# Two halved norms: GpSimd makes one half of slot 1's weight remainder, the vector engine the other, and slot 1's matmuls follow all of slot 0's

## The reference, cut to what matters

```
x  = x  + 0.5 * gate * swiglu(modulate(rms_norm(x,  g), shift, scale), w_in, w_out)   # latent tokens
xc = xc + 0.5 * gate * swiglu(modulate(rms_norm(xc, g), shift, scale), w_in, w_out)   # context tokens
hx = modulate(rms_norm(x, g1), ...);  hc = modulate(rms_norm(xc, g1), ...)
q, k, v = split(h @ w_qkv)      # differential attention: q of the latents, k and v of both
```

## Time and profile before

| | before |
|---|---|
| median of 3 runs | 2273.41 us (2270.28 to 2276.93) |
| the profiled execution | 2277.63 us, span 2274.6 us |
| TensorE busy | 2234.0 us (98%) |
| vector engine busy | 1460.7 us (64%) |
| ScalarE busy | 847.1 us (37%) |
| GpSimd busy | 161.4 us (7%) |
| granted TensorE clock | 0.993 of full speed |

### The profile page before, as it was taken

One profiled execution on the slowest core, in us unless ns is written; L12 is line 12 of the kernel. 1 busy time (PEld: TensorE's weight loads), 2 busy tenths in 40 slices (PEclk: granted clock), 3 DMA queues, 4 the chain that ended last, 5 costly groups with the idle time before them and its releaser, 6 DMA issues.

```text
span 2274.6 us, 37311 instructions
## 1 busy us (share of the span) xinstructions
PE 2234.0 (98%) x14124; PEld 2009.0 (88%) x14124; DVE 1460.7 (64%) x2305; ACT 847.1 (37%) x1133; POOL 161.4 (7%) x235
## 2 busy tenths in 40 slices
PE   8999999999999999999999999999999999999998
PEld 8999999999999988888988888898888888788998
DVE  4657886555788777678777767873333346556555
ACT  4445344444635432122432212232212234445443
POOL 0100000130000100010001001100000001000000
PEclk9999999998999999999999999999999999999999
DMA  6325664323665555455245555533232223113453
GB/s 229 113 80 207 207 229 155 135 78 120 211 239 185 194 194 179 175 191 178 91 149 201 171 177 193 175 116 111 79 106 102 81 95 130 56 57 131 179 201 136
DMA packets 65482, 343.19 MB, mean 151 GB/s; under 512 B 7152, under 2 KB 10480, under 8 KB 42608
## 3 DMA queue, kind: packets, MB, share of 16 engines
q1 hardware_dynamic: 44656, 266.47, 33.4%
q0 software_dynamic: 20736, 75.51, 9.9%
HBM read 340.90 MB, written 1.05 MB: 150 GB/s over the span
## 4 chain that ended last, share of the span: by engine, by line
PE 81%; issue 11%; DVE 4%; ACT 3%; DMA 1%; POOL 0%; DVEq 0%; SPq 0%; ACTq 0%; POOLq 0%
PE gpt L868 20%; PE gpt L869 20%; PE gpt L870 20%; ACT w_hi L1492 2%; DVE w_lo L1999 1%; PE gpt L967 1%; PE mbt L1150 1%; PE gpt L789 1%; PE gpt L790 1%; PE gpt L791 1%; PE gpt L968 1%; PE gpt L969 1%; PE mbt L1409 1%; PE gpt L1367 1%; PE gpt L1368 1%
## 5 line engine op out<-in xcount | busy, mean ns | idle before, releaser
L868 PE MATMUL gpt<-xn_hi,w_hi 128*128 128x512 f32 (+2 forms) x2256 | 745.3, 330 | 6.4 <-DVE midf L2210 3.6
L870 PE MATMUL gpt<-xn_hi,w_lo 128*128 128x512 f32 (+2 forms) x2256 | 740.8, 328 | 0.0
L869 PE MATMUL gpt<-xn_lo,w_hi 128*128 128x512 f32 (+2 forms) x2256 | 740.8, 328 | 0.0
L1999 DVE TENSOR_TENSOR w_lo<-raw,w_hi 128x2048 fp32r<-128x2048 f32 (+2 forms) x277 | 560.8, 2025 | 238.7 <-ACT w_hi L1492 238.7
L1492 ACT ACTIVATE w_hi<-raw 128x2048 fp32r<-128x2048 f32 (+2 forms) x277 | 471.2, 1701 | 368.5 <-PE gpt L870 324.7
L868 PEld LDWEIGHTS gpt<-xn_hi,w_hi 128*128 128x128 f32 x2256 | 426.1, 189 | 47.4 <-DVE midf L2210 6.0
L870 PEld LDWEIGHTS gpt<-xn_hi,w_lo 128*128 128x128 f32 x2256 | 426.2, 189 | 37.2
L869 PEld LDWEIGHTS gpt<-xn_lo,w_hi 128*128 128x128 f32 x2256 | 425.4, 189 | 37.6
L868 PE MATMUL gpt<-mid_hi,w_hi 128*128 128x512 f32 (+2 forms) x996 | 331.3, 333 | 5.2 <-DVE mid_lo L2215 4.0
L869 PE MATMUL gpt<-mid_lo,w_hi 128*128 128x512 f32 (+2 forms) x996 | 330.0, 331 | 0.0
L870 PE MATMUL gpt<-mid_hi,w_lo 128*128 128x512 f32 (+2 forms) x996 | 330.0, 331 | 0.0
(11 more groups left out here) (345 smaller groups left out, 2706.8 us busy)
## 6 DMA issues: line engine op xcount, KB each, us to landing
raw<-in_up_a SPq DMA_DIRECT2D x72, 1024.0 KB, 4.8
ada_w<-in_ada POOLq DMA_DIRECT2D x144, 512.0 KB, 3.5
raw<-in_up_b SPq DMA_DIRECT2D x60, 1024.0 KB, 4.7
raw<-in_down_a SPq DMA_DIRECT2D x48, 768.0 KB, 4.3
raw<-in_down_b SPq DMA_DIRECT2D x48, 640.0 KB, 3.9
raw<-in_win SPq DMA_DIRECT2D x16, 1024.0 KB, 4.9
raw<-in_qkv SPq DMA_DIRECT2D x12, 1024.0 KB, 4.8
raw<-in_wout SPq DMA_DIRECT2D x8, 1024.0 KB, 4.8
```

Of the source, the lines that this page charges most:

```text
L868: mm(o, wh[b][:, j, :], hi(k), start=(k == 0), stop=False)
L869: mm(o, wh[b][:, j, :], lo(k), start=False, stop=False)
L870: last = mm(o, wl[b][:, j, :], hi(k), start=False, stop=(k == kt - 1))
L1999: V.tensor_tensor(wl[b][:, 0:tiles, :], raw[b][:, 0:tiles, :], wh[b][:, 0:tiles, :].bitcast(F32), ALU.subtract).then_inc(lo_ready, 1)
```

## The change: what it does

GpSimd gets a new step, `second_low`, between its two powers at norms 7 and 8: when ScalarE has rounded slot 1, it subtracts the half of the remainder with k below 4 (128x1024). The vector engine's whole remainder of slot 1 goes; instead it makes the other half, `second_split`, behind latent tile 7, after a wait for GpSimd's half. Its order becomes: remainders of tiles 2 and 3 with tiles 4 and 5, the context half's means, tiles 6 and 7, its half of the remainder, the context tiles. TensorE does all of slot 0 first, with the context half's columns in its middle, then slot 1 with tiles 0 to 3 after a wait for GpSimd's half, the context half's rows, and slot 1 with tiles 4 to 7 after a wait for the vector engine's half. Norm 6 keeps the old order.

```
             def half_powers(ni, low=None):
                 for c in range(2):
+                    if c == 1 and low is not None:
+                        second_low(low)
...
+            def second_low(s):
+                pool.wait_ge(hi_ready, s + 1)
+                nc.gpsimd.tensor_tensor(by_k(w_lo[1], 0), by_k(raw[1], 0), by_k(w_hi[1], 0).bitcast(F32), ALU.subtract)\
+                    .then_inc(second_lo, 1)
...
-            half_powers(7)
-            half_powers(8)
+            half_powers(7, S_F4 + 1)
+            half_powers(8, S_QKV + 1)
...
                 if after != POOL_NORM:
                     half_columns(after, 1)
-                else:
-                    pool_sums(1, range(6, KT))
+                    gemm_part(0, hi, lo, 0, range(4, KT), xn_ready, r0, done)
+                    pe.wait_ge(second_lo, after - 6)
+                    pe.wait_ge(evac_done, free_at(2 * p + 1))
+                    gemm_part(1, hi, lo, 0, range(0, 4), xn_ready, r0)
+                    half_rows(after, 1)
+                    pe.wait_ge(lo_ready, done_at(2 * p + 1))
+                    gemm_part(1, hi, lo, 0, range(4, KT), xn_ready, r0, done)
+                    return
+                pool_sums(1, range(6, KT))
...
+            def second_split(p, n):
+                dve.wait_ge(second_lo, n)
+                V.tensor_tensor(by_k(w_lo[1], 1), by_k(raw[1], 1), by_k(w_hi[1], 1).bitcast(F32), ALU.subtract).then_inc(lo_ready, 1)
...
-            norm2_half(7, 0, range(2, KT // 2), 4)
-            split(S_F4 // 2, 1, SIDE_T)
+            norm2_half(7, 0, range(2, KT - 2), 4)
             half_columns(7, 1)
-            norm2_half(7, 0, range(KT // 2, KT))
+            norm2_half(7, 0, range(KT - 2, KT))
+            second_split(S_F4 // 2, 1)
             norm2_half(7, 1, range(KT))
```

More of the change, by code:

```diff
@@ L264, in build @@
         first_hi, first_lo = sem("first_hi"), sem("first_lo")
-        k_hi, k_lo = sem("k_hi"), sem("k_lo")
+        k_hi, k_lo, second_lo = sem("k_hi"), sem("k_lo"), sem("second_lo")
         half_done, res_x, xq_ready, xs_used = sem("half_done"), sem("res_x"), sem("xq_ready"), sem("xs_used")
@@ L653, in _, with half_powers @@
             load_ada(2)
-            def half_powers(ni):
+            def second_low(s):
+                pool.wait_ge(hi_ready, s + 1)
+                nc.gpsimd.tensor_tensor(by_k(w_lo[1], 0), by_k(raw[1], 0), by_k(w_hi[1], 0).bitcast(F32), ALU.subtract)\
+                    .then_inc(second_lo, 1)
+            def half_powers(ni, low=None):
                 for c in range(2):
+                    if c == 1 and low is not None:
+                        second_low(low)
                     pool.wait_ge(hpart_ready, half_chain(ni, c) + 1)
@@ L2721, in _ @@
                 late=[lambda w=w: derive(1, w) for w in range(3)])
-            norm2_half(7, 0, range(2, KT // 2), 4)
-            split(S_F4 // 2, 1, SIDE_T)
+            norm2_half(7, 0, range(2, KT - 2), 4)
             half_columns(7, 1)
-            norm2_half(7, 0, range(KT // 2, KT))
+            norm2_half(7, 0, range(KT - 2, KT))
+            second_split(S_F4 // 2, 1)
             norm2_half(7, 1, range(KT))
             ffn(S_F4 // 2, 4, T2, gated_residual(1, 0, T2), [SIDE_T, SIDE_T], 8, 3)
-            norm2_half(8, 0, range(2, KT // 2), 4)
-            split(S_QKV // 2, 1, SIDE_T)
+            norm2_half(8, 0, range(2, KT - 2), 4)
             half_columns(8, 1)
-            norm2_half(8, 0, range(KT // 2, KT))
+            norm2_half(8, 0, range(KT - 2, KT))
+            second_split(S_QKV // 2, 2)
             norm2_half(8, 1, range(1))
```

## The result

The changed kernel took 2287.4 us in the median of 9 runs (2282.07 to 2292.78), the kernel before, on the same chip, 2275.55 (2270.28 to 2280.65). The ratio is 1.0049, with a 95% interval of 1.0034 to 1.0064: 11.2 us slower, 7.7 to 14.6.

A forecast was written before the change was run, and what follows sets the result against it. TensorE, busy 98%, bounds the kernel, so only its pauses count. 2.8 us without a collision plus 2 x 1.9 of hold make 6.6 us slower: 2280.0 on the runs' median, own range 2277 to 2284, outer range 2274.0 to 2287.0.

The forecast's parts named there:

- The hold: Norms 7 and 8: GpSimd's half holds the vector engine's tile 2 remainder, 1.9 us each; whole hold 0.70.
- my four multiplies: Length of GpSimd's 128x1024 half, taken as four 128x256 multiplies: 2.5 us.
- Norm 8's restart: Second query slot: TensorE goes on 6.39 us after the context half's rows, 2.5 us later than before.
- the late rows: Norm 8: second half's rows, moved behind 24 more matmuls, set the chain to the query slot; 2.5 us.
- Norm 7 without the collision: Ahead of the fourth feed-forward: the new order gives nothing back, costing 0.2 us plus 0.1 at the context tiles.
- the collision: Norms 7 and 8: GpSimd's half and tile 2's remainder contend, lengthening TensorE's pause; 2 x 1.9 us.
- A partial hold: Rival: the vector engine slips in between GpSimd's pieces; half the hold, 4.7 us slower; chance 0.15 with no hold.
- no hold: Rival: GpSimd's half doesn't hold tile 2's remainder; 2.8 us slower, 2276.2; chance 0.15 with a partial hold.
- A far slower GpSimd: Rival: rounded output doubles GpSimd's half to 5 us, holding 4.4 at each norm; 11.7 us slower; chance 0.10.
- The faster one: Rival: with w_lo off the vector engine, 2.21 us go at both norms; 4.4 us less, 2269.0; chance 0.05.
- That the change doesn't act: Rival: late ScalarE rounding moves the hold to tile 3 at about the same price; counted in the first case.
- the bound between them: About 0.3% (6.8 us), what a measurement can tell from no change; the forecast lay just inside.

The follow-up runs named there:

- experiment 1: The changed kernel with GpSimd's half given back to the vector engine, TensorE's new order kept; ratio 1.0025 to the kernel before.
- experiment 3: The changed kernel with nine unused keep_clock calls filling TensorE's pause between tiles 1 and 2; ratio 1.0023 to the kernel before.
- experiment 2: The kernel before, old order, with slot 1's remainder cut in two and the first half on GpSimd; ratio 1.0040 to the kernel before.
- experiment 5: experiment 1 with the second half's rows made right behind slot 0's last tile; ratio 0.9998 to the kernel before.
- experiment 6: The kernel before with two unused vector-engine subtractions ahead of tile 2's remainder, no GpSimd half; ratio 1.0034, 7.7 us slower.

## Why the prediction was right and wrong

**The hold: right, sizes a little high.** GpSimd's half took 2.34 (I took 2.5). It held tile 2's remainder for 1.72 (I had 1.9) and lengthened the pause by as much. The Trainium skill (SBUF — State Buffer, "Who interferes with whom") says that the first to issue keeps the shared ports for the whole instruction; the trace agrees, as the remainder lost 1.72 of the 1.92 us that it stood beside one GpSimd instruction of 2.34. The estimate of 2.25, half of what the Trainium skill (GPSIMD Engine Reference, "Elementwise — side-by-side cycle accounting") has for 2048 elements, was nearer than my four multiplies.

**Norm 8's restart: right.** 6.40 from the rows to the restart (6.39 forecast), an idle of 2.91 (about 3), and 2.7 us for the late rows by experiment 1 (2.5).

**Norm 7 without the collision: right within what can be read.** Its stretch grew by 5.2 (15.24 to 20.4, from the first latent matmul to the context matmuls); 1.72 of hold and 3.3 of clock leave 0.2, and 0.3 was forecast.

**The step that failed** is this sentence of the collision: "TensorE already stands waiting for this very remainder, so all of it lengthens the pause, at both norms, and all that follows slides." What follows does not slide, it stretches: half clock behind the pause cost 3.3 us at norm 7 (experiment 3) and 3.4 at norm 8 (experiment 1), and behind the restart 1.5 more (1903.22 to the next copies at 1910.76 is 7.54; before, 1892.62 to 1898.68 is 6.06). The sum had no term for the clock at all, though the row for the pause of before stood in front of me, the mean granted clock of that kernel was 0.993, and its trace has a stretch at half clock (0.60 in the mean from 509 to 526). With it the account closes: 3.4 of hold, 2.7 of rows, 6.7 of clock and 0.2 make 13.0 of the 13.1 us between norm 7's rounding and the query slot; the hold and the rows alone make 6.3 with that 0.2, near my 6.6. Over the runs the change costs 11.2, less than the 14.6 of these two traces. That other executions had less half clock at these places is likely, as the table of pauses varies, but it isn't shown. The Trainium skill (TensorE: Matmul & The Clock Gate, "Part 1: The HAM clock gate") puts it so: "the default state is throttled, and activity releases the throttle". The traces agree in that half clock stood behind 7 of 8 long empty pauses and behind none of 6 filled ones. They also show that a pause of one length doesn't settle it: after the same 3.34 us it came at one norm and not at the other (experiment 2).

**What was luck.** Put on the median that I forecast from, the measured ratio is 2284.6 us. That is above the forecast's own range, 2277 to 2284, and inside the outer one only because that went up to 2287.0 for a slow GpSimd, which didn't occur.

**The rivals.** A partial hold and no hold fall: the remainder lost 1.72 of 1.92. A far slower GpSimd comes nearest in time, at 11.7 us, and falls by its own row, 2.34 and not 5. The faster one falls with experiments 1 and 5, where the remainder is off the vector engine's way ahead of tile 4 and GpSimd makes none of it: 1.0025 and 0.9998. That the change doesn't act falls too.

**The chances.** I put 0.53 on no measurable change and 0.44 on slower, because the sum lay 0.2 us inside the bound between them. All that I had left out had one sign, since the clock stood at 1.00 there and could only fall; that should have moved the weight to slower, which is what was measured.

**Open.** The runs don't tell what decides between half and full clock behind a pause of 1.6 us (4 of 14), nor why half clock lasts 3 us in one case and 10 in another. Experiments 1 and 2 add to 0.65% where the change has 0.49; the intervals are too wide to say whether the two costs overlap.

## What to carry to other kernels

Where TensorE is the bound, price a longer pause twice: its length, and the same matmuls at half clock behind it. In the profiled execution this cost twice as much as the pause had grown; over the runs of experiment 6 it was about one and a half times as much (4.7 for 3.0). Before work is given to an idle engine, look at what the other engines do with two SBUF operands in those microseconds, and at who stands waiting for it. And where an order is rewritten, look for the small instruction that is moved along with the large ones: four row matmuls were the loss of the new order.

## What the runs showed of the hardware

- A GpSimd subtraction of 128x1024 with an fp32r output took 2.34 to 2.39 us; the vector engine makes the same half in 1.22 us.
- A vector instruction with two SBUF operands that usually takes 0.48 us took 2.20 when it began 0.42 behind a GpSimd instruction of 2.34, on tiles that the latter neither reads nor writes. The next vector instruction, with one operand in PSUM, took its usual 0.48.
- TensorE at half clock reads as 100% busy. Only the granted clock, the count in a stretch (15 to 17 against 28 in 3 us) or the pitch of the matmuls (0.21 against 0.12 us) tells it from work.
